# A transformer pair on one core: block-attention heads set between projection blocks, full-width attention tiles, a shorter rotary front

## The chip, the cores and the metric

The kernel runs on one core of one Trainium2 chip. The time is device microseconds (us) of one execution, smaller is better; given is the median of three runs. Engines: PE (TensorE; PEld is its weight load), DVE (VectorE), ACT (ScalarE), POOL (GpSimd) and SP, which issues loads.

## The reference

Two transformer blocks over 256 tokens of width 1024 (16 meta tokens stand before them as keys, 272 in all). The first block has latent attention (MLA, 8 heads, 64 plain and 32 rotary features), differential attention (4 heads of two maps) and a mixture of 16384 experts. The second has a hybrid mixer, cross attention over a memory of 256 and a convolutional FFN. What the change touches:

```
q = rmsnorm(c_q @ w_uq); k = rmsnorm([k_nope, k_rope])
q, k = [nope, rope(rotary part)]        # t1*cos - t2*sin, t1*sin + t2*cos
y_mla = softmax(q k^T * s + mask) v     # 8 heads, 272 keys
y_diff = (softmax(q1 k1^T) - lam * softmax(q2 k2^T)) v     # 4 heads
proj = h @ w_in_2                       # 3200 columns: conv 768, moba q,k,v 1536, gla 896
y_conv = c_b * dwconv(c_c * c_h);  y_moba = softmax(causal, alibi) v     # 8 heads
x = x + [y_conv, y_moba, y_gla] @ w_out_2
x = x + cross_attention(rmsnorm(x) * g)
```

## The kernel before, in words

Activations lie feature-major: 128 features on the partitions, 256 tokens (272 in the front) along the row. Every weight matrix is cut into blocks of 128x1024 that SP loads into `raw`, a ring of four (`RING`). Each block is split into two float32r parts: ACT makes `w_hi` (L717), and POOL or DVE, by `lo_owner`, makes `w_lo` (L588, L1219). `project` (L1926) multiplies a block with eight operand tiles, three products each (hi·hi, lo·hi, hi·lo), so a block is 24 passes of PE. Products go by turns to PSUM banks 0 and 1 and are taken from there by DVE or ACT (`bank_free`). Each engine's order is written out by hand; semaphores join them.

**Front** (`project_in`, 17 blocks of 272 columns). Between its blocks stand: the query product of the 8 MLA heads from `w_uq` (L2063), the values (`values`, L2027), the rotary turn of the queries by a constant matrix (`spread` with `rot`, L1970), the keys, four heads at a time in 64 columns (`keys`, L2035, twice), the turn of the shared rotary key (L2092), and the keys' sums of squares (L2096, L2098). POOL multiplies all queries with the cosines (L661); DVE multiplies the turned ones with the sines and adds (L1322, L1326), the same for the key (L1330, L1333). The memory's norm (L851, L1307) runs beside them.

**Attention** (`attention` on each engine, `walk` gives the steps). In step s PE computes `scores(s+1)` (L2178), `weigh(s-2)` (L2220) and `turn(s-1)` (L2198, transposes of the probabilities). DVE makes the row maximum (`soft_in`), the inverse of the sum and the lower part of a finished head (`finish`, L1442); ACT the exponential (L904), the copy of turned probabilities (L913) and the upper part of a head (`head_out`, L925); POOL scales by the inverse (`normalise`, L626). `key_tiles` cuts the 272 keys into tiles of 128, 128 and 16 rows, and transposes of a causal tile are cut to 32 rows. Values of an MLA, block ("moba") or cross head are 64 columns wide.

**Mixer** (`project_in2`, 25 blocks in the order `IN2_ORDER`). The gated linear attention ("gla") runs between the first blocks. The convolution on DVE (L1778 to L1786) follows blocks 16 to 18, the scores of the first two block heads stand after blocks 21 and 22, and the other steps of the eight heads come when all 25 blocks are done. Their outputs go into `x_op`, the operand that the 25 blocks read. Two pieces of output block 0 (`first_out2`) stand in the last two steps. Then come output blocks 0 to 7, the sum of squares (`mixed_sum`, L1961, L1963), the eight operand tiles of cross attention (`gained_hi`, L753 on ACT, `gained_lo`, L1250 on DVE) all behind the last output block, and the query blocks of cross attention.

## Time and profile before

| | |
|---|---|
| time, median of 3 runs | 1409.96 us (1407.91 to 1410.04) |
| the profiled execution | 1411.54 us, span 1409.4 us |
| busy | PE 98%, PEld 88%, DVE 69%, ACT 48%, POOL 53% of the span |
| mean granted PE clock | 0.993 |
| chain that ended last | PE 88%, DVE 5%, ACT 2%, POOL 2%, issue 2% |

The span is from the first to the last instruction; some 2 us lie around it. A row of the timeline gives start, length, engine, line, operation and shapes; 128*64 before the operand is the part of the array in use, rows by columns. One float32 matmul is two rows of PE. The length of a row holds the modelled end of its last matmul, so lengths are read here from one start to the next. In brackets stands the idle time ahead and what ended it.

### The profile page before, as it was taken

How to read it: one execution, taken by the hardware profiler on the slowest of the kernel's cores; microseconds unless marked ns; L12 is line 12 of the kernel's file. 1: busy time of each engine (PE TensorE's matmuls, PEld its weight loads, DVE VectorE, ACT ScalarE, POOL GpSimd, SP SyncE). 2: the span in 40 equal slices, each digit the busy share in tenths (PEclk: the TensorE clock that was granted, in tenths of full speed). 3: DMA queues.
4: the chain of work that ended last, by engine and by line, in shares of the span. 5: the costliest groups of instructions: out<-in, count | busy, mean ns of one | idle time of the engine just before them, and what ended most of it. 6: DMA issues, size and time to landing. Idle time of an engine off the chain costs nothing.

```text
span 1409.4 us, 28595 instructions
## 1 busy us (share of the span) xinstructions
PE 1377.3 (98%) x9810; PEld 1244.9 (88%) x9810; DVE 970.2 (69%) x1690; ACT 681.1 (48%) x1044; POOL 743.8 (53%) x606
## 2 busy tenths in 40 slices
PE   9999999999999999999999999999999988899997
PEld 8777689999999999988888888999999967799996
DVE  6724659999888888766666665544455754798886
ACT  6433665445555555533333333444465356555553
POOL 5423268888777667644444444444434535455441
PEclk9999999999999999999999999999999999999999
DMA  7511156667655555567777776555544513465552
GB/s 300 162 47 45 65 171 208 189 203 225 206 184 185 177 181 184 184 220 238 237 227 237 238 230 205 197 189 180 183 172 136 178 54 112 135 190 181 179 179 75
DMA packets 89801, 249.67 MB, mean 177 GB/s; under 512 B 9976, under 2 KB 35848, under 8 KB 89100
## 3 DMA queue, kind: packets, MB, share of 16 engines
q1 hardware_dynamic: 88260, 243.20, 53.3%
q10 hardware_dynamic: 1480, 5.65, 1.1%
q8 instruction: 40, 0.66, 0.2%
q14 instruction: 21, 0.17, 0.0%
HBM read 234.64 MB, written 15.25 MB: 177 GB/s over the span
## 4 chain that ended last, share of the span: by engine, by line
PE 88%; DVE 5%; ACT 2%; POOL 2%; issue 2%; DMA 0%; ACTq 0%; DVEq 0%; SPq 0%; POOLq 0%
PE ps L1926 45%; PE ps L2376 25%; PE ps L2363 4%; PE ps L2346 3%; POOL w_lo L588 2%; PE ps L2220 1%; PE ps L2178 1%; PE ps L2198 1%; PE ps L2148 1%; DVE w_lo L1219 1%; PE ps L2000 1%; PE ps L2035 1%; ACT w_hi L717 1%; PE ps L1941 1%; DVE big L1255 0%
## 5 line engine op out<-in xcount | busy, mean ns | idle before, releaser
L588 POOL TENSOR_TENSOR w_lo<-raw,w_hi 128x512 fp32r<-128x512 f32 x514 | 679.4, 1343 | 536.8 <-ACT w_hi L717 532.6
L1926 PE MATMUL ps<-x_op,w_hi 128*128 128x256 f32 (+1 forms) x3824 | 711.4, 287 | 6.4 <-DVE x_op L1250 3.3
L1926 PEld LDWEIGHTS ps<-x_op,w_hi 128*128 128x128 f32 x3824 | 597.0, 191 | 19.7 <-issue 9.0
L717 ACT ACTIVATE w_hi<-raw 128x1024 fp32r<-128x1024 f32 x399 | 420.0, 1055 | 273.5 <-PE ps L2376 206.4
L1926 PE MATMUL ps<-x_op,w_lo 128*128 128x256 f32 (+1 forms) x1912 | 541.2, 283 | 0.0
L1926 PEld LDWEIGHTS ps<-x_op,w_lo 128*128 128x128 f32 x1912 | 365.8, 191 | 0.0
L2376 PE MATMUL ps<-w_hi,h_op 128*128 128x512 f32 x1008 | 280.7, 395 | 0.0
L1219 DVE TENSOR_TENSOR w_lo<-raw,w_hi 128x1024 fp32r<-128x1024 f32 x141 | 183.3, 1300 | 83.4 <-ACT w_hi L717 82.9
L2376 PEld LDWEIGHTS ps<-w_hi,h_op 128*128 128x128 f32 x1008 | 187.4, 188 | 43.1
L2376 PE MATMUL ps<-w_lo,h_op 128*128 128x512 f32 x504 | 158.6, 395 | 0.0
L1621 DVE TENSOR_TENSOR work<-route_t,ps 128x1536 bf16<-128x1536 bf16 x64 | 112.3, 1754 | 8.7
L2376 PEld LDWEIGHTS ps<-w_lo,h_op 128*128 128x128 f32 x504 | 94.7, 188 | 23.0
L1648 DVE CAST h_op<-ps 128x256 fp32r<-128x256 f32 x128 | 54.4, 425 | 81.2 <-PE ps L2376 72.4
L1001 ACT ACTIVATE kv_mem<-ps 128x256 f32<-128x256 f32 x98 | 37.5, 383 | 133.1 <-PE ps L1926 133.1
L1617 DVE TENSOR_TENSOR route_t<-kept,ps 128x1024 bf16<-128x1024 f32 x64 | 78.2, 1222 | 30.9 <-PE ps L2346 27.1
L1641 DVE TENSOR_TENSOR ps<-work,big 128x256 f32<-128x256 f32 x124 | 54.3, 438 | 35.6 <-ACT work L1042 33.6
L2363 PE MATMUL ps<-h_op,w_hi 128*128 128x256 f32 x368 | 66.3, 280 | 1.7 <-DVE h_op L1856 1.7
L626 POOL TENSOR_TENSOR big<-big 128x256 f32<-128x256 f32 (+3 forms) x48 | 26.2, 567 | 70.5 <-DVE big L1417 70.5
L2363 PEld LDWEIGHTS ps<-h_op,w_hi 128*128 128x128 f32 x368 | 56.4, 188 | 2.1 <-DVE h_op L1856 1.2
L1650 DVE TENSOR_TENSOR h_op<-ps,h_op 128x256 fp32r<-128x256 f32 x128 | 54.4, 425 | 4.4
L2346 PE MATMUL ps<-work,route_t 128*128 128x128 bf16 x768 | 54.0, 220 | 0.2 <-DVE work L1621 0.2
L2363 PE MATMUL ps<-h_op,w_lo 128*128 128x256 f32 x184 | 51.7, 281 | 0.0
(332 smaller groups left out, 1264.7 us busy)
## 6 DMA issues: line engine op xcount, KB each, us to landing
raw<-blocks SPq DMA_DIRECT2D x403, 512.0 KB, 3.7
early_store<-kv_mem SPq DMA_DIRECT2D x96, 128.0 KB, 1.7
work<-early_store SPq DMA_DIRECT2D x96, 128.0 KB, 3.9
big<-consts SPq DMA_DIRECT2D x1, 1336.0 KB, 8.8
big<-consts ACTq DMA_DIRECT2D x1, 1336.0 KB, 5.4
big<-h_t ACTq DMA_DIRECT2D x4, 272.0 KB, 5.1
big<-bias_lines SPq DMA_DIRECT2D x8, 136.0 KB, 4.4
bias_lines<-bias_lines SPq DMA_DIRECT2D x1, 1056.0 KB
```

What stands on the lines that cost most here:

```text
L588: ins = pool.tensor_tensor(w_lo[:, s, half], raw[:, s, half], w_hi[:, s, half].bitcast(F32), ALU.subtract)
L717: act.activation(w_hi[:, s, :], raw[:, s, :], ACT.Copy).then_inc(sem("hi_done"), 1)
L1219: dve.tensor_tensor(w_lo[:, s, :], raw[:, s, :], w_hi[:, s, :].bitcast(F32), ALU.subtract).then_inc(sem("lo_dve"), 1)
L1617: dve.tensor_tensor(marks[:, m:m + 2], con("iota").unsqueeze(1).unsqueeze(1).to_broadcast([P, 2, 4, P]), routed[:, m:m + 2, tok].unsqueeze ...
L1621: dve.tensor_tensor(scaled[:, m], marks[:, 1].unsqueeze(1).to_broadcast([P, 3, 4, P]), routed[:, 3:6, tok].unsqueeze(3).to_broadcast([P, 3 ...
L1641: dve.tensor_tensor(weighted[:, b, :], a, G[:, bass.ds(chunk.value(), 1), :].rearrange("p e t -> p (e t)"), ALU.mult).then_inc(sem("act_us ...
L1648: dve.tensor_copy(h_op[:, b, 0, :], weighted[:, b, :]).then_inc(sem("act_hi"), 1)
L1650: dve.tensor_tensor(h_op[:, b, 1, :], weighted[:, b, :], h_op[:, b, 0, :].bitcast(F32), ALU.subtract).then_inc(sem("acts_ready"), 1)
L1926: mm = pe.matmul(ps[:, m_bank, 0:T], w, xp, start=(k == 0 and j == 0), stop=(k == last and j == 2))
L2346: mm = pe.matmul(ps[:, 2 + j % 2, P * k:P * k + P], marks[:, 2 * (j % 2), k, :], scaled[:, j % 2, r, k, :], start=(r == 0), stop=(r == 2))
L2363: mm = pe.matmul(out, w, x, start=(first and j == 0 and k % 2 == 0), stop=(last and j == 2), skip_group_check=True)
L2376: mm = pe.matmul(ps[:, 4 + 2 * t + half, :], h_op[:, b, h, rows], w[:, s, 512 * half:512 * (half + 1)], start=(first and j == 0), stop=Fal ...
```

## The change

- `w_uq` has 128 columns per head: 96 as before and the 32 rotary ones once more in turned order; the front's block 4 likewise. The turned features fall out of the products, so both multiplications with `rot` go. ACT copies the turned rows (32 partitions), DVE multiplies them with gain and signed sines, multiplies the straight ones with the cosines and adds, all on 32 partitions. POOL's multiplication goes. `w_uq` grows from 768 to 1024 KB.
- `keys` makes two heads per matmul, once; the keys' sums of squares take pairs. The gain of the plain key features moves into `key_scale`. The wait for the memory's root stands one matmul group later.
- Tiles of keys are always 128 wide: the third one overlaps the second and its values are zero in the overlap (`tail`). Transposes are 128x128, values 128 columns (a pair of heads; the half that is not wanted is not read).
- Mixer: `IN2_ORDER` brings the block heads' queries and keys ahead of the convolution's inputs. The scores of heads 0 and 1 stand after blocks 14 and 15; each of the eight steps of attention has one projection block (17 to 24) in it. Block heads write into `first_op`, an own buffer, and both halves of bank 7. A head's `weigh` waits until the one before it has been read (`outputs_out`). The convolution stands in steps 6 to 8 of DVE. Output block 0 is cut into tiles (6,7), (2,3), (4), (0,1), (5). POOL and ACT split one block per step.
- Cross attention's operand tiles are made one by one behind each residual.

```diff
-IN2_ORDER = [24, 18, 19, 20, 21, 22, 23, 14, 15, 16, 17, 0, 1, 2, 3, 4, 5, 6, 10, 7, 11, 8, 12, 9, 13]
+IN2_ORDER = [24, 18, 19, 20, 21, 22, 23, 14, 15, 16, 17, 6, 10, 7, 11, 2, 8, 12, 3, 9, 13, 4, 5, 0, 1]
...
-                yield j, min(P, units[u]["keys"] - P * j), first, at
+                yield j, min(P * j, units[u]["keys"] - P), first, at
...
+        def out_at(o, rows=slice(0, P), first=0):
+            if 0 <= o - HEADS - DH < MH:
+                return ps[rows, 7, (o % 2) * NQ + first:(o % 2 + 1) * NQ]
+            return ps[rows, 7 if o % 2 == 0 else 1, first:NQ]
...
-            pool.tensor_tensor(rope_a[:, :, 0:NQ], q_mla,
...
+            for i in range(MH):
+                los(B_FILL + 2 + i, B_FILL + 3 + i)
+                normalise(U_MOBA + i, U_MOBA + i + 1)
...
+            act.activation(flat2(rope_p), banks(4, 4)[QK:P, :], ACT.Copy).then_inc(sem("q_raw"), 1)
...
+            for i, (s, p, o) in enumerate(walk(U_MOBA, U_X)):
+                if s is not None and i >= 2:
+                    soft(s)
+                his(min(B_FILL + 4 + i, B_OUT2 + RING))
+                if i == 3:
+                    mix_hi(0, y_gla, 6)
+                if i == 9:
+                    mix_hi(1, conv_y, 0)
+                if o is not None:
+                    head_out(o)
+                if p is not None:
+                    probs_out(p)
...
                 act.wait_ge(sem("bank_free"), M_OUT2 + j + 1)
+                gained_hi(R_XATTN, "xattn", (j,))
                 squares(res[:, j, :], j, NQ)
...
+            for i, (s, p, o) in enumerate(walk(U_MOBA, U_X)):
+                if i >= 3:
+                    finish(U_MOBA + i - 3)
+                if p is not None and i >= 3:
+                    inverse(p)
+                if s is not None and i >= 2:
+                    soft_in(s)
+                if 1 <= i <= 8:
+                    evacuate_in2(16 + i)
+                if i == 5:
+                    mix_lower(0, y_gla, 6)
...
-                pe.wait_ge(sem("y_hi"), o - 1)
-                pe.wait_ge(sem("y_ready"), outputs_read(o))
+                one = 0 < o - HEADS - DH <= MH
+                pe.wait_ge(sem("y_hi"), o - 1 + one)
+                pe.wait_ge(sem("y_ready"), outputs_read(o) + one)
...
+            def fill_moba(s, p):
+                if s is not None:
+                    project_in2(17 + s - U_MOBA)
+                elif p is not None:
+                    pe.wait_ge(sem("mix_lo"), 1)
+                    first_out2((6, 7))
+                    moba_done(4)
+                    first_out2((2, 3))
+                else:
+                    moba_done(6)
+                    first_out2((4,))
+            attention(U_MOBA, U_X, 2, fill_moba)
+            pe.wait_ge(sem("mix_lo"), 2)
+            first_out2((0, 1))
+            moba_done(MH)
+            first_out2((5,))
```

**Where instructions move.** PE in the front, between projection blocks 7 and 12 (`...` stands for blocks); before:

```order
L1970 MATMUL ps<-big 96x512 x4
...
L2027 MATMUL ps<-big 16x512 x2
...
L2035 MATMUL ps<-big 64x272 x8
...
L2092 MATMUL ps<-big 96x272
L2096 MATMUL ps<-big,ones 8x272
L2098 MATMUL ps<-big 8x272 x8
```

and now:

```order
L2040 MATMUL ps<-big 128x512 x2
...
L2046 MATMUL ps<-big 128x272 x8
...
L2101 MATMUL ps<-big,ones 8x272
L2103 MATMUL ps<-big 8x272 x4
```

Both turns are gone; the group of key products stood twice and stands once, at full width; the sums are halved.

PE in one step of the block heads, between the scores of one head and the transposes of another; before:

```order
L2178 MATMUL ps<-big 128x128
L2178 MATMUL ps<-big 128x256
L2220 MATMUL ps<-big 64x256
L2220 MATMUL ps<-big 64x128
L2198 MATMUL ps<-kept,big 128x128 x3
```

and now, with the 24 passes of a projection block between scores (L2184) and `weigh` (L2226):

```order
L2184 MATMUL ps<-big 128x128
L2184 MATMUL ps<-big 128x256
L1944 MATMUL ps<-x_op,w_hi 128x256 x2
L1944 MATMUL ps<-x_op,w_lo 128x256
...
L2226 MATMUL ps<-big 128x256
L2226 MATMUL ps<-big 128x128
L2204 MATMUL ps<-kept,big 128x128 x3
```

The same step is longer by a block, and there are eight such blocks fewer ahead of the heads.

DVE in step 6 of the block heads now: `finish` (L1450), inverse, row maximum, a lower part (L1227), a block taken from PSUM (L1725), then half the convolution (L1800 to L1806), which before stood between blocks 17 and 18 without a head beside it:

```order
L1450 TENSOR_TENSOR first_op<-ps,first_op 64x256
L1425 RECIPROCAL big<-big 128x2
L1408 SCALAR_TENSOR_TENSOR big<-big,ps 128x128
L1408 SCALAR_TENSOR_TENSOR big<-big,ps 128x256
L1417 TENSOR_REDUCE big<-big 128x1 x2
L1419 TENSOR_SCALAR big<-big 128x2
L1227 TENSOR_TENSOR w_lo<-raw,w_hi 128x1024
L1725 SCALAR_TENSOR_TENSOR big<-ps,big 128x256
L1800 TENSOR_TENSOR big<-big 128x512
L1804 TENSOR_SCALAR big<-big,par 128x256
L1806 SCALAR_TENSOR_TENSOR big<-big,par 128x255
L1806 SCALAR_TENSOR_TENSOR big<-big,par 128x254
```

The convolution moved from the projection's stretch into the heads' steps, behind the row maximum.

## Rows read from the trace of the kernel before

**Rows 1.** DVE's groups, 1086 to 1128: busy, mean ns, idle ahead and its end.

```profile
L1219 DVE TENSOR_TENSOR w_lo<-raw,w_hi 128x1024 fp32r<-128x1024 f32 x7 | 9.2, 1308 | 0.1
L1719 DVE SCALAR_TENSOR_TENSOR big<-ps,big 128x256 f32<-128x256 f32 x14 | 5.9, 423 | 10.9 <-PE ps L1926 10.9
```

**Rows 2.** Busy time by stretch: length, PE, PEld, DVE, ACT, POOL, clock, DMA.

```profile
45.00:97.20 52.20, 50.82 (x305) 37.61 (x303) 23.00 (x18) 21.53 (x35) 15.88 (x9) 1.00 0.32 107
1127.30:1151.20 23.90, 19.84 (x93) 12.45 (x92) 14.24 (x47) 13.51 (x43) 6.37 (x12) 0.86 0.07 23
1141.10:1147.90 6.80, 6.22 (x22) 4.08 (x21) 2.32 (x9) 2.95 (x10) 2.31 (x5) 0.50 0.00 0
```

**Rows 3.** Timeline of PE in the front, projection blocks mostly left out.

```profile
48.02 3.70 PE L2027 MATMUL ps<-big 128*128 128x512 f32 x8 [0.92 <-ACT big L851]
...
54.58 3.60 PE L1970 MATMUL ps<-big 96*96 96x512 f32 x8
57.61 0.81 PE L1926 MATMUL ps<-x_op,w_hi 128*128 128x272 f32 x2
...
66.17 3.89 PE L2035 MATMUL ps<-big 128*64 128x272 f32 x16
...
80.25 0.69 PE L2092 MATMUL ps<-big 32*96 32x272 f32 x2
...
81.42 3.83 PE L2098 MATMUL ps<-big 64*8 64x272 f32 x16
```

**Rows 4.** Timeline of DVE and of POOL in the same stretch.

```profile
54.82 6.72 DVE L1219 TENSOR_TENSOR w_lo<-raw,w_hi 128x1024 fp32r<-128x1024 f32 x1
...
54.46 4.74 POOL L661 TENSOR_TENSOR big<-big 96x2048 f32<-96x2048 f32 x1 [2.80 <-issue]
```

**Rows 5.** Timeline of PE ahead of attention and in one MLA step.

```profile
115.25 1.04 PE L2277 MATMUL ps<-kept,big 128*128 128x128 f32 x8
116.13 1.28 PE L1977 MATMUL ps<-ones 128*128 128x128 f32 x10
...
129.91 1.14 PE L2220 MATMUL ps<-big,work 128*64 128x256 f32 x6
130.99 1.00 PE L2198 MATMUL ps<-kept,big 128*128 128x128 f32 x5
131.92 0.97 PE L2178 MATMUL ps<-big 128*128 128x144 f32 x4
```

**Rows 6.** Timeline of PE: projection block 12, steps of the block heads, output block 0.

```profile
1087.14 0.48 PE L1926 MATMUL ps<-x_op,w_hi 128*128 128x256 f32 x2
...
1090.10 0.40 PE L1926 MATMUL ps<-x_op,w_hi 128*128 128x256 f32 x2
...
1129.17 0.92 PE L2178 MATMUL ps<-big 64*128 64x128 f32 x4
1130.02 0.86 PE L2220 MATMUL ps<-big 128*64 128x256 f32 x4
1130.81 0.55 PE L2198 MATMUL ps<-kept,big 128*128 128x128 f32 x3
...
1139.51 0.55 PE L2198 MATMUL ps<-kept,big 128*128 128x128 f32 x3 [1.29 <-POOL big L626]
...
1151.28 0.50 PE L1926 MATMUL ps<-x_op,w_hi 128*128 128x256 f32 x2 [0.93 <-DVE x_op L1442]
```

**Rows 7.** Timeline of DVE in the convolution, and of POOL beside it.

```profile
1104.10 1.01 DVE L1783 SCALAR_TENSOR_TENSOR big<-big,par 128x255 f32<-128x255 f32 x2
...
1105.92 2.97 DVE L1783 SCALAR_TENSOR_TENSOR big<-big,par 128x255 f32<-128x255 f32 x2
...
1105.89 2.72 POOL L588 TENSOR_TENSOR w_lo<-raw,w_hi 128x512 fp32r<-128x512 f32 x2 [2.83 <-ACT w_hi L717]
```

**Rows 8.** Timeline of PE: first query blocks of cross attention, and the scores behind.

```profile
1175.77 0.47 PE L1926 MATMUL ps<-x_op,w_hi 128*128 128x256 f32 x2 [0.16 <-DVE x_op L1250]
...
1180.62 1.14 PE L2178 MATMUL ps<-big 64*128 64x256 f32 x8
```

More of the change, by code:

```diff
@@ L852, in _ @@
             evacuate_in(6)
+            act.activation(xf[0:QK, 0:HEADS * NQ], banks(4, 4)[0:QK, :], ACT.Square).then_inc(sem("q_squares"), 1)
             evacuate_in(7)
@@ L1796, in _ @@
+            mix_lower(1, conv_y, 0)
+            finish(U_X - 1)
             for k in range(KT):
@@ L1914, in arrived, with project @@
                 pe.wait_ge(*rest_taken(n))
-            def project(n, m_bank, T=NQ, free=None, ready=None, tiles=range(KT), last=KT - 1, x=x_k):
-                if 0 in tiles:
+            def project(n, m_bank, T=NQ, free=None, ready=None, tiles=range(KT), last=KT - 1, x=x_k, first=0):
+                if first in tiles:
                     arrived(n)
@@ L1925, in project @@
                     for j, (w, xp) in enumerate(parts(n.mod(RING), k * P, k * P + P, x(0, k, T), x(1, k, T))):
-                        mm = pe.matmul(ps[:, m_bank, 0:T], w, xp, start=(k == 0 and j == 0), stop=(k == last and j == 2))
+                        mm = pe.matmul(ps[:, m_bank, 0:T], w, xp, start=(k == first and j == 0), stop=(k == last and j == 2))
                 if last in tiles:
@@ L2022, in values @@
             def values(t):
-                rows = min(P, NK - P * t)
+                key = min(P * t, NK - P)
                 if t == 2:
@@ L2026, in values, with keys @@
                 for k in range(2):
-                    mm = pe.matmul(ps[0:rows, 2 + t % 2, :], ckvn[:, k, P * t:P * t + rows], w_ukv[:, k, 512:1024],
-                                   start=(k == 0), stop=(k == 1))
+                    mm = pe.matmul(ps[:, 2 + t % 2, :], ckvn[:, k, key:key + P], w_ukv[:, k, 512:1024], start=(k == 0), stop=(k == 1))
                 mm.then_inc(sem("v_product"), 1)
-            def keys(w):
-                for h in range(4):
+            def keys():
+                for pair in range(HEADS // 2):
                     for k in range(2):
-                        a = NOPE * (4 * w + h)
-                        mm = pe.matmul(ps[0:NOPE, 4 + h, 0:NK], w_ukv[:, k, a:a + NOPE], ckvn[:, k, :], start=(k == 0), stop=(k == 1))
+                        mm = pe.matmul(ps[:, 4 + pair, 0:NK], w_ukv[:, k, P * pair:P * pair + P], ckvn[:, k, :], start=(k == 0), stop=(k == 1))
                 mm.then_inc(sem("k_product"), 1)
@@ L2271, in _ @@
             for t in range(3):
-                rows = min(P, NK - P * t)
+                key = min(P * t, NK - P)
                 if t == 2:
@@ L2537, in cross_out, with first_heads @@
                     mm.then_inc(sem("block_used"), 1)
-            def first_heads(part):
+            def first_heads(s, p):
+                if s is not None:
+                    return
+                part = 0 if p is not None else 1
                 pe.wait_ge(sem("y_ready"), HEADS + DH + MH + 2)
@@ L2616, in constants @@
     half = ROPE // 2
-    rot = np.zeros((QK, QK))
-    for j in range(half):
-        rot[NOPE + half + j, NOPE + j] = -1.0
-        rot[NOPE + j, NOPE + half + j] = 1.0
-    put("rot", rot)
     freq = np.float32(10000.0) ** (-np.arange(half, dtype=np.float32) / np.float32(half))
@@ L2703, in layout @@
     put("final", lay("final_norm_g_2"))
+    put("tail", (np.arange(P) >= 2 * P - (NK - P)).astype(np.float32))
+    for k, source in enumerate(("mla_qk_norm_q", "mla_qk_norm_k")):
+        put("qkp", np.concatenate([np.zeros(NOPE, np.float32), lay(source)[0][turned]]), k)
     for name, source in (("dq", "diff_q_norm"), ("dk", "diff_k_norm"), ("gla", "gla_norm_g_2")):
```

255 lines of the change are left out of this document (118 added, 137 removed).

## The prediction

> **What bounds the kernel now.** I read the page's engines and chain first: PE is busy 98% of the span and carries 88% of the chain that ended last (both in the table of the profile), so a change pays where it takes passes from PE or a wait from in front of it. Then the groups of DVE in the mixer's projection: its evacuation of a block waited 10.9 us for PE and never the reverse, and one lower part costs it 1.3 us, one evacuation 0.42 [rows 1]. Then the busy time by stretch: in the front PE works 50.8 of 52.2 us while DVE works 23.0 and POOL 15.9; in the stretch of the block heads it works only 19.8 of 23.9, at a mean granted clock of 0.86, and within it from 1141.1 to 1147.9 at 0.50, that is at 1.2 GHz [rows 2]. So the front is short of nothing but passes, and the block heads are the one place where PE starves and then also runs slowly. Last come the timelines, for the length of every piece that changes. All sums are against the profiled execution of 1411.54 us; the median of the runs is 1.6 us below it, and I take that off at the end.
>
> **A. Front ahead of attention: -10.1 us.** Removed from PE, each from its start to the next one's: the turn of the queries, 54.58 to 57.61, 3.0 us; one of two groups of key products, 16 rows from 66.17, 3.8 us; the turn of the shared key, 80.25 with one more product behind it, 0.6; half of the keys' sums, which ran from 81.42 for 3.8 us, 1.9 [rows 3]. The values waited 0.92 us for ACT's root (L851) [rows 3]; the wait now stands behind a group of half that length, 1.6 us, which covers it. Together 10.3. The products with `w_uq` keep their time though their columns go from 96 to 128: a row's length follows what streams through, since 16 rows take 3.89 us at 64 columns and 16 take 3.83 at 8 [rows 3]. Added off PE: a copy on ACT (2048 columns, which took POOL 4.74 us with a second input [rows 4]; ACT works 21.5 of 52 us [rows 2], so it has room for even that); three operations of DVE on 32 partitions in place of two on 96, and `key_scale` with a gain more. DVE has 29 us free of 52 here [rows 2], so they cost nothing but the last one, where PE waited for it closely; I charge 0.2 for this (0 to 0.5). POOL's 4.74 us multiplication goes; beside it one lower part on DVE took 6.72 us instead of 1.3 [rows 4, 1]. PE did not wait for it, hence 0, but the cover grows. `w_uq` is 256 KB longer; the DMA engines are busy to 0.32 at 107 GB/s here [rows 2], so this is 2.4 us of a queue that idles most of the time; 0, at worst a quarter of it, 0.6. Bounds of A: -9.0 to -10.8.
>
> **B. Attention front: -4.8 us.** A step of an MLA head lasts 2.9 us on PE, from `weigh` at 129.91 over the transposes at 130.99 and the scores at 131.92 to 132.8 [rows 5]. Its pure work at full width: one row of 128x128 takes 0.11, eight taking 0.88 from 115.25 to 116.13 [rows 5]. Five transposes are then 0.55; scores of 416 columns in two rows each 0.69; `weigh` of 448 columns 0.75; in all 2.0. Before, the transposes took 0.93 and `weigh` 1.08 since array shapes changed at 64 columns, 32 rows and 16 rows. I do not book the whole 0.9. `weigh` of a head waits for the output of the one before it to be read, which waits for ACT's `head_out` and DVE's `finish`, and the transposes for POOL's scaling. No row parts what of the 0.9 is this loop and what shape, so I take the middle, 2.5: 8 x 0.4 = 3.2. The four differential heads lose about 0.4 each in the same way: 1.6. Bounds of B: 0, if the other engines' chain sets the step already, to -8.8, if all changes of shape go.
>
> **C. Mixer: -7.5 us.** Before, from block 12's first pass (1087.14) to the end of output block 0 it takes 65.6 us: its second half begins at 1151.28, and 12 passes of 0.12 end it at 1152.7 [rows 6]. Eight groups of three passes take 1087.14 to 1090.10, 2.9 a block [rows 6]. Now PE has there: 13 blocks, 37.8; eight scores of 0.85 (1129.17 to 1130.02), 6.8; eight `weigh`, now at the shape of the projection, hence 768 columns in all at 0.11 per 128, 0.65 instead of 0.79, 5.1; eight times three transposes of 0.11, 2.6; output block 0, 2.9 [rows 6, 5]. Sum 55.2. What is not hidden: the last two heads have no projection block behind them, only pieces of output block 0, and the loop `weigh`, `head_out`, `finish` that ended in waits of 1.29 and 0.93 [rows 6] stands once more at the tail; 1.1. DVE is late in step 6: its share per head is 14.24 us over eight, 1.8 [rows 2], with 0.42 and 1.3 for evacuation and lower part 3.5, and half the convolution adds 1.3 to 1.5 alone and up to 3.7 beside POOL (a pair of L1783 takes 1.01 us alone, 2.97 beside a 2.72 us lower part of POOL [rows 7]). That makes 7 us in a step in which PE has 2.9 + 0.85 + 0.65 + 0.33 = 4.7 of work, with a step of slack in the PSUM banks; 1.7. Total 58.1, so -7.5. The half clock goes too: with a projection block in every step PE has no row of short waits such as it had before 1141. Bounds of C: -5.0 with every step 0.3 longer and the tail at 2, -9.2 with nothing late but the tail.
>
> **D. Cross attention: -0.8 us.** The first one and a half query blocks ran 1175.77 to 1180.62, 4.85 us for 36 passes that cost 4.32, and waited 0.16 for DVE's lower parts of the operand [rows 8]. With the tiles made behind each residual both losses go, and a little of the wait ahead. Against it: `squares` now stands behind a gain on ACT, which I put at one operation of such a size, 0.4 us [rows 1]. Bounds of D: -2 to +0.3.
>
> **Sum.** -10.1 - 4.8 - 7.5 - 0.8 = -23.2: 1388.3 for a profiled execution, 1386.8 against the median. Below, "the same" means within 0.2%, 2.8 us, about what a measurement of this kernel can tell from no change.
>
> **Rivals.** *R1, DVE sets the block heads' step.* DVE now carries evacuation, lower parts, convolution and soft heads in one queue, and POOL's lower parts run beside them. If contention as in [rows 7] meets it in most steps (3.5 becomes 5.5, PE's 4.7 is exceeded by 0.8 in six of the eight), C gains 2.7 only: 1391.6. For it: 2.97 against 1.01. Against it: POOL works 6.4 of 23.9 us here [rows 2], and its share per step only grows by half a lower part. The Trainium skill, "SBUF — State Buffer", section on the two separate sides, says that DVE with two SBUF inputs and GpSimd exclude each other for a whole instruction; by that rule DVE waits out each lower part of POOL that it meets, and [rows 7] agree. Chance 0.14.
>
> *R2, attention's front is set by the other engines.* DVE, ACT and POOL pass one head's data in turn, and PE only fills in; then a shorter PE step becomes a longer wait ahead of transposes or `weigh`, and B is 0: 1391.6. For it: the 0.93 us of five transposes hold at most 0.4 of shape changes and may be such a wait already [rows 5]. Against it: no release is named at these rows. Chance 0.10.
>
> *R3, slower.* `finish` stands first in DVE's step; until PE has weighed and ACT has copied the head, the lower part and the evacuation behind it stand still, and PE's next block needs both. One such round, a head's share, lower part and evacuation, is 3.5 us by C; PE sits out nothing as long as it is under 4.7 plus the 2.9 of one block that is ready ahead. From 7.6 us on PE waits each step. To lose the 23 us of all terms, eight steps would have to be 7.6 + 3.5 us, 11 us each; at 11.5 us the result is 1413. Lower parts of 6.72 us [rows 4] in place of 1.3 would come near. Chance 0.04.
>
> *R4, the change doesn't take out what it says.* Both turns and one key group are gone from the order of instructions, so this leaves only a front whose loads or ACT become late: half of A, 1392. Chance 0.04.
>
> **Numbers.** The forecast, all four terms about as worked out, has 0.68. It, R1, R2 and R4 lie between 1378 and 1398: the low end has B and C each some 4 us better than booked, the high end R1 and R2 together with A at its lower bound. Own range of the forecast: 1380 to 1391. Faster by over 0.2%: 0.94; the same 0.02; slower 0.04.
>
> **What the profile of the changed kernel would show.** A: no row of the turns, one group of key products, PE's work ahead of attention about 10 us shorter, no row of DVE's lower part near 6.7 us beside it. B: 2.5 us from `weigh` to `weigh`; 2.9 speaks for R2, 2.1 for my low end. C: granted clock 1.0 across the block heads, a step of 4.7 to 5 us, short waits at the transposes, a wait at projection block 22 or 23 behind DVE's evacuation. A step over 5.5 us with PE's wait ended by DVE in most steps is R1; over 7.6, R3. D: 36 passes in 4.3 us. I would be wrong most likely by the attention front, whose loop I could not separate from its shape changes, or by the half clock, if PE falls to 1.2 GHz elsewhere.

## The result, and the profile after

The changed kernel takes 1392.63 us (median of 4 runs, 1391.68 to 1393.47) against 1409.58 us for the kernel before (4 runs, 1407.91 to 1410.04); the ratio is 0.9882 with a 95% interval of 0.9865 to 0.9899. It is 17.0 us faster where 23.2 were forecast. It lies within the stated range of 1378 to 1398, but outside the forecast's own range of 1380 to 1391. The profiled executions differ by 18.1 us (1411.54 to 1393.47, spans 1409.4 and 1391.3), and their difference can be laid out stage by stage, by the starts of the same matmuls on PE in both:

| stretch of PE | before | after | change | booked |
|---|---|---|---|---|
| start to the first sum over ones in the front (19.30; 16.58) | 19.30 | 16.58 | -2.7 | none |
| from there to attention's first memory transposes (115.25; 101.60) | 95.95 | 85.02 | -10.9 | A, -10.1 |
| attention, to the residual's operand (182.25; 163.67) | 67.00 | 62.07 | -4.9 | B, -4.8 |
| experts, to block 12 of the mixer (1087.14; 1069.13) | 904.89 | 905.46 | +0.6 | none |
| block 12 to the end of output block 0 (1152.72; 1131.44) | 65.58 | 62.31 | -3.3 | C, -7.5 |
| output blocks 1 to 7, to the sum of squares (1174.47; 1154.49) | 21.75 | 23.05 | +1.3 | D |
| to cross attention's scores (1183.90; 1164.81) | 9.43 | 10.32 | +0.9 | D, -0.8 |
| the rest | 225.5 | 226.5 | +1.0 | none |

The first line is no effect of the change, as the repeated profiles below show. From block 12 to the end the profiles take 322.3 us before and 322.2 after, and the repeated pair below takes 322.3 and 322.2 again: what the mixer gains is lost behind it. In these profiles the whole gain stands ahead of the experts.

The page of the changed kernel, busy time by engine: all shares as before within one per cent.

```profile
PE 1358.2 (98%) x9776; PEld 1245.2 (89%) x9776; DVE 972.9 (70%) x1691; ACT 681.7 (49%) x1045; POOL 738.4 (53%) x605
```

PE in the front, which answers to [rows 3]:

```profile
59.19 3.84 PE L2046 MATMUL ps<-big 128*128 128x272 f32 x16
...
69.56 2.00 PE L2103 MATMUL ps<-big 128*8 128x272 f32 x8
```

One group of key products stands where two stood, with as many rows as one of them had, and the sums of squares take 2.0 instead of 3.8 us.

PE in two steps of MLA, to be set against [rows 5]:

```profile
115.24 1.01 PE L2226 MATMUL ps<-big,work 128*128 128x256 f32 x6
116.09 0.74 PE L2204 MATMUL ps<-kept,big 128*128 128x128 f32 x5
116.67 0.87 PE L2184 MATMUL ps<-big 128*128 128x144 f32 x4
117.46 1.11 PE L2226 MATMUL ps<-big,work 128*128 128x256 f32 x6
118.48 0.76 PE L2204 MATMUL ps<-kept,big 128*128 128x128 f32 x5
```

From one `weigh` to the next it is 2.22, then 2.42 us, against 2.9. The transposes' share went from 0.93 to 0.58, that of the scores from 0.90 to 0.79.

The mixer by stretch (length, PE, PEld, DVE, ACT, POOL, clock, DMA), to be set against [rows 2]: the heads' steps with a block in each, the heads' tail, the first query blocks of cross attention, and a piece of its attention.

```profile
1077.90:1116.90 39.00, 39.00 (x284) 34.94 (x284) 26.49 (x62) 20.38 (x48) 18.87 (x21) 1.00 0.33 110
1117.20:1131.40 14.20, 9.95 (x68) 8.46 (x66) 11.55 (x23) 6.54 (x15) 6.42 (x7) 1.00 0.38 119
1154.50:1161.50 7.00, 7.00 (x40) 6.53 (x40) 2.88 (x4) 2.50 (x5) 2.52 (x2) 0.76 0.62 204
1174.00:1177.50 3.50, 3.50 (x18) 3.10 (x18) 0.21 (x1) 2.01 (x4) 3.45 (x4) 0.63 0.00 0
```

For 39 us PE does not miss a beat; then, in the tail of 14.2 us, it works 9.95 and DVE 11.55. The half clock has left the heads' steps, but stands now in the query blocks and in cross attention.

PE in the middle of the heads' steps, in their tail and behind the output blocks (projection rows mostly left out), to be set against [rows 6, 8]:

```profile
1096.68 0.81 PE L2226 MATMUL ps<-big 128*128 128x256 f32 x4
1097.34 0.49 PE L2204 MATMUL ps<-kept,big 128*128 128x128 f32 x3
1097.76 0.92 PE L2184 MATMUL ps<-big 64*128 64x128 f32 x4
1101.58 0.81 PE L2226 MATMUL ps<-big 128*128 128x256 f32 x4
...
1120.51 0.89 PE L2226 MATMUL ps<-big 128*128 128x256 f32 x4 [0.21 <-DVE first_op L1450]
...
1124.86 0.89 PE L2226 MATMUL ps<-big 128*128 128x256 f32 x4 [0.93 <-DVE first_op L1450]
1126.91 0.55 PE L2204 MATMUL ps<-kept,big 128*128 128x128 f32 x3 [1.16 <-POOL big L633]
...
1128.04 0.92 PE L2226 MATMUL ps<-big 128*128 128x256 f32 x4 [0.23 <-ACT big L917]
1130.36 0.50 PE L1944 MATMUL ps<-first_op,w_hi 128*128 128x256 f32 x2 [1.40 <-DVE first_op L1456]
...
1146.29 0.51 PE L1944 MATMUL ps<-first_op,w_hi 128*128 128x256 f32 x2 [0.47 <-POOL w_lo L595]
...
1154.49 0.70 PE L1974 MATMUL ps<-big,ones 128*128 128x256 f32 x2 [2.27 <-POOL big L618]
...
1161.52 1.14 PE L2184 MATMUL ps<-big 64*128 64x256 f32 x8
```

A step is 4.90 us (1096.68 to 1101.58) without a wait. In the tail some 4 us of waits stand in brackets, ended by DVE's `finish`, POOL's scaling and the lower part of the convolution's output (L1456). All PE waits from block 12 to the end of output block 0 add up to 4.3 us, before to 4.4: they have moved to the tail and are not fewer. Ahead of the sum of squares PE waits 2.27 us for POOL (1.33 before), and it waits 0.47 for a lower part of POOL once more.

### The profile page after: what moved, and what is told of

It is laid out like the page before. It is cut to its first block, busy times and chain, and to the rows that moved or that the text cites. A ratio compares the mean times of both kernels' runs of the same rounds, so it can differ in the third digit from the quotient of the medians.

```text
span 1391.3 us, 28517 instructions
## 1 busy us (share of the span) xinstructions
PE 1358.2 (98%) x9776; PEld 1245.2 (89%) x9776; DVE 972.9 (70%) x1691; ACT 681.7 (49%) x1045; POOL 738.4 (53%) x605
## 4 chain that ended last, share of the span: by engine, by line
PE 88%; DVE 6%; ACT 2%; issue 2%; POOL 1%; DMA 1%; ACTq 0%; DVEq 0%; SPq 0%; POOLq 0%
PE ps L1944 47%; PE ps L2382 25%; PE ps L2369 4%; PE ps L2352 3%; PE ps L2184 1%; PE ps L2226 1%; ACT w_hi L720 1%; DMA raw<-blocks 1%; PE ps L2152 1%; PE ps L2204 1%; DVE w_lo L1227 1%; DVE big L1249 1%; PE ps L1959 1%; DVE big L1263 1%; PE ps L2320 1%
## 5 line engine op out<-in xcount | busy, mean ns | idle before, releaser
L1944 PE MATMUL ps<-x_op,w_hi 128*128 128x256 f32 (+1 forms) x3696 | 689.2, 287 | 5.4 <-DVE x_op L1258 3.5
L1944 PEld LDWEIGHTS ps<-x_op,w_hi 128*128 128x128 f32 x3696 | 577.5, 191 | 18.6 <-issue 9.0
L1944 PE MATMUL ps<-x_op,w_lo 128*128 128x256 f32 (+1 forms) x1848 | 523.4, 283 | 0.0
L1944 PEld LDWEIGHTS ps<-x_op,w_lo 128*128 128x128 f32 x1848 | 353.7, 191 | 0.0
L1227 DVE TENSOR_TENSOR w_lo<-raw,w_hi 128x1024 fp32r<-128x1024 f32 x141 | 180.3, 1279 | 88.2 <-ACT w_hi L720 87.7
```

The costliest lines, as they stand in the source:

```text
L1227: dve.tensor_tensor(w_lo[:, s, :], raw[:, s, :], w_hi[:, s, :].bitcast(F32), ALU.subtract).then_inc(sem("lo_dve"), 1)
L1944: mm = pe.matmul(ps[:, m_bank, 0:T], w, xp, start=(k == first and j == 0), stop=(k == last and j == 2))
```

## The experiments

All times are medians, and the stretches are read from each run's own profile. The stretch "mixer" is from block 12's first pass to the sum of squares: 87.3 before, 85.4 after.

**The changed kernel again.** No edit.

> The changed kernel once more, unaltered, for what repeats. Theory 1 (the clock's dips have places): the stretch at half clock stands again behind the last output block (36 passes of the first query blocks in about 6.1 us, where 4.3 would be full clock), PE idles again some 4 us between 1117 and 1131, and the front has none. Theory 2 (the dips fall by chance): the query blocks' length differs by over 1 us from 6.1, or the front of projections behind 13 us shows a half-clock stretch of 1.5 us or more, and the time moves with it. Time 1392.6 +- 1.

Measured: 1392.09 us (1390.18 to 1395.12). The mixer takes 85.36 us, to the hundredth what the first profile of this kernel has, with nearly the same waits (0.21, 0.98, 1.16, 1.41, 2.48) and the same 6.1 us for 36 passes. The front is another matter. Busy time by stretch of this run (first the front, then the query blocks):

```profile
12.00:16.00 4.00, 3.86 (x17) 3.86 (x18) 3.95 (x5) 1.78 (x4) 2.87 (x2) 0.50 1.00 397
1156.00:1162.00 6.00, 5.91 (x32) 5.55 (x33) 2.68 (x4) 2.60 (x5) 2.56 (x3) 0.72 0.69 230
```

So theory 1 holds for the mixer, theory 2 for the front: the same program runs from 12 to 16 us at 1.2 GHz in one execution and at 2.4 GHz in another. The profiled execution is the slowest of the four at a mean clock of 0.993, the fastest has 0.998, so the later dips need not stand in every execution either.

**The kernel before again.** No edit.

> The kernel before once more, for what repeats in it. If the half-clock stretch of the front (12 to 18 us) falls by chance, its length may differ by 1 us or more from the first profile of it; the time from block 12's first pass to the sum of squares is 87.3 us with the dip in the block heads at 1141, about 85.3 if that dip falls elsewhere. The waits for POOL's scaling in the heads' steps (0.65, 1.29) and the 1.33 ahead of the sum of squares repeat within 0.2 us.

Measured: 1410.52 us (1408.39 to 1411.82). Its front and its block heads by stretch:

```profile
12.00:16.00 4.00, 3.92 (x30) 3.81 (x30) 3.96 (x6) 2.29 (x3) 2.98 (x2) 1.00 1.01 405
1140.00:1148.00 8.00, 7.42 (x31) 5.01 (x30) 2.54 (x10) 3.59 (x12) 2.31 (x5) 0.57 0.01 2
```

This time the front of the kernel before has the full clock, and its first sum over ones starts at 16.87 us instead of 19.30. The -2.7 in the first line of the table is therefore no effect of the change. Like is compared with like by the stretch from that sum to attention's first transposes: with the dip ahead of it 95.96 us before and 84.28 after, without it 96.91 and 85.02, so the change takes 11.7 or 11.9 us and not 10.9. Some 0.7 to 1.0 us of the dip's cost is thus made up again before attention. The mixer takes 87.30 us, and its dip repeats, with the waits of 0.66 and 1.30 ahead of it.

**Projection blocks ahead of the heads again.** The interleaving alone is undone.

```diff
-            project_in2(16)
+            project_in2(16, 9)
...
                 if s is not None:
-                    project_in2(17 + s - U_MOBA)
+                    return
...
+            los(B_FILL + 2, B_OUT2 + 2)
             for i in range(MH):
-                los(B_FILL + 2 + i, B_FILL + 3 + i)
...
             soft(U_MOBA + 1)
+            his(B_OUT2 + 2)
...
-            evacuate_in2(16)
+            evacuate_in2(18)
             inverse(U_MOBA + 1)
+            evacuate_in2(24)
```

> The changed kernel with the interleaving alone undone: projection blocks 17 to 24 stand ahead of the heads' steps again, with their evacuations and lower parts; own buffer, halves of bank 7, full-width tiles, the cut of output block 0 and the convolution in steps 6 to 8 are kept. Theory 1 (a block in each step covers the loop over the other engines): PE waits in most steps, 4 us or more in the mixer, time 3.5 to 6 us above the changed kernel's, 1396 to 1398. Rival (the wait at the tail is the same either way and the interleaving moves it only): within 1.5 us of the changed kernel's.

Measured: 1398.57 us (1396.94 to 1399.43), mixer 91.8 us, 6.5 more than with a block in each step. PE in its steps, and the stretch by clock:

```profile
1113.91 0.89 PE L2228 MATMUL ps<-big 128*128 128x256 f32 x4
1114.94 0.55 PE L2206 MATMUL ps<-kept,big 128*128 128x128 f32 x3
1115.42 0.92 PE L2186 MATMUL ps<-big 64*128 64x128 f32 x4
1117.75 0.89 PE L2228 MATMUL ps<-big 128*128 128x256 f32 x4 [1.41 <-ACT big L917]
1118.90 0.79 PE L2206 MATMUL ps<-kept,big 128*128 128x128 f32 x3 [0.27 <-POOL big L633]
1119.62 1.65 PE L2186 MATMUL ps<-big 64*128 64x128 f32 x4
...
1128.73 1.62 PE L2228 MATMUL ps<-big 128*128 128x256 f32 x4 [1.45 <-DVE first_op L1451]
```

```profile
1118.00:1132.00 14.00, 12.28 (x42) 9.16 (x42) 10.64 (x34) 7.14 (x23) 3.77 (x8) 0.54 0.00 1
```

After one wait of 1.41 us every group takes nearly double (scores 1.65 for 0.92), until blocks come again. Of the 6.5 us only 0.8 is more waiting (5.1 us against 4.3 to the end of output block 0, in five places of over 0.25 us and not in most steps, as theory 1 had it); by far the most is the clock, at half speed for some 15 us. What the blocks in the steps keep up is the clock, more than they cover waits. The time to the end shows even less of it: this profile has no dip behind the mixer, and from block 12 to the end it takes 325.8 us against 322.2.

**Without the taps of the convolution.** This version leaves the filter out, so its output is not the reference's.

```diff
-                if i in (6, 7):
-                    t = i - 6
-                    w = [pcol("scw", 3 * t + j) for j in range(3)]
-                    step(dve.tensor_scalar(conv_y[:, t, :], conv_u[:, t, :], w[2], pcol("scb", t), ALU.mult, ALU.add))
-                    for back in (1, 2):
-                        step(dve.scalar_tensor_tensor(out=conv_y[:, t, back:NQ], in0=conv_u[:, t, 0:NQ - back], scalar=w[2 - back],
-                                                      in1=conv_y[:, t, back:NQ], op0=ALU.mult, op1=ALU.add))
...
-                    dve.tensor_tensor(flat2(conv_y), flat2(conv_y), flat2(proj2[:, 0:2, :]), ALU.mult)
+                    dve.tensor_tensor(flat2(conv_y), flat2(conv_u), flat2(proj2[:, 0:2, :]), ALU.mult)
```

> Leaves out the three taps of the convolution per half on DVE (2.8 us of DVE in steps 6 and 7 of the block heads); the last product reads the product of the inputs in place of the filtered one. Theory 1 (the convolution stands in front of finish and makes the heads' last steps late): PE's idle time from projection block 23 to the end of output block 0, 4.3 us in the changed kernel, falls to 2.5 or less, time 1390 to 1391. Rival (the loop of weigh, head_out, finish and the scaling at the tail, where no projection block is left to cover it): idle time stays at 3.6 or more, time within 0.7 us of the changed kernel's.

Measured: 1390.9 us (1389.43 to 1392.85), 1.2 below the changed kernel in the same series; mixer 83.81, 1.55 less. The waits on `finish` (0.21 and 0.98) are gone, one of 0.57 for ACT's copy stands in their place, and those of 1.16 for POOL, 0.23 and 1.41 at the end stay. The tail's waits still add up to 3.4 us, between the bounds of the two theories. So both have a part: some 1.5 us are the convolution's, 2.5 and more are not.

**The convolution's first half early.**

```diff
-IN2_ORDER = [24, 18, 19, 20, 21, 22, 23, 14, 15, 16, 17, 6, 10, 7, 11, 2, 8, 12, 3, 9, 13, 4, 5, 0, 1]
+IN2_ORDER = [24, 18, 19, 20, 21, 22, 23, 14, 15, 16, 17, 6, 10, 7, 11, 2, 4, 8, 12, 9, 13, 3, 5, 0, 1]
...
-                            pe.wait_ge(sem("bank_free"), M_IN2 + (13, 15, 18, 21)[h // 2])
+                            pe.wait_ge(sem("bank_free"), M_IN2 + (13, 15, 19, 21)[h // 2])
...
-                if i == 6:
-                    dve.wait_ge(sem("bank_free"), M_IN2 + 23)
-                    step(dve.tensor_tensor(flat2(conv_u), flat2(proj2[:, 2:4, :]), flat2(proj2[:, 4:6, :]), ALU.mult))
-                if i in (6, 7):
-                    t = i - 6
+                if i in (2, 6):
+                    t = i // 6
+                    dve.wait_ge(sem("bank_free"), M_IN2 + (17, 23)[t])
+                    step(dve.tensor_tensor(conv_u[:, t, :], proj2[:, 2 + t, :], proj2[:, 4 + t, :], ALU.mult))
+                if i in (2, 7):
+                    t = i // 7
```

> The inputs of the convolution's first half are projected as blocks 15 and 16, and that half (product and taps) is done in step 2 of DVE, where it has 12 of 39 us free; the second half's product stays in step 6, its taps stand in step 7. All work is kept. Theory 1: as without taps in its size: 1.5 to 2 us of idle time go, time 1390.5 to 1391.5, if step 2 has the room; PE has no new wait in steps 2 to 4. Rival (the loop at the tail): no change within 0.7 us. A third way: step 2 becomes late itself and PE waits ahead of weigh or turn there, 1 us lost.

Measured: 1389.78 us (1389.26 to 1390.31), the range all but below that of the changed kernel in the same series; mixer 83.62, 1.74 less, with all work kept. PE in its tail:

```profile
1123.24 0.89 PE L2227 MATMUL ps<-big 128*128 128x256 f32 x4 [0.40 <-DVE first_op L1450]
1125.29 0.55 PE L2205 MATMUL ps<-kept,big 128*128 128x128 f32 x3 [1.16 <-POOL big L633]
1126.42 0.92 PE L2227 MATMUL ps<-big 128*128 128x256 f32 x4 [0.23 <-ACT big L917]
1128.75 0.51 PE L1945 MATMUL ps<-first_op,w_hi 128*128 128x256 f32 x2 [1.41 <-DVE first_op L1456]
```

The wait of 0.21 is gone and that of 0.93 has become 0.40, as without the taps; step 2 had the room. What is left are waits of the last two heads for ACT, DVE and POOL, which no projection block covers; the two longest of them are looked into at R1 below.

**Gains behind all output blocks again.** The last part of the change is undone, on ACT and on DVE.

```diff
                 act.wait_ge(sem("bank_free"), M_OUT2 + j + 1)
-                gained_hi(R_XATTN, "xattn", (j,))
                 squares(res[:, j, :], j, NQ)
+            act.wait_ge(sem("block_used"), B_XQ)
+            gained_hi(R_XATTN, "xattn", range(KT))
...
-                if k:
-                    gained_lo(R_XATTN, "xattn", (k - 1,))
-            gained_lo(R_XATTN, "xattn", (KT - 1,))
+            dve.wait_ge(sem("bank_free"), M_XQ)
+            gained_lo(R_XATTN, "xattn", range(KT))
```

> Only the last part of the change is undone: the operand tiles of cross attention are made behind all eight output blocks again. Theory 1 (the gains between the output blocks delay ACT's upper parts and squares and through them POOL): PE's wait ahead of the sum of squares falls from 2.27 to about 1.3 us; the first query blocks wait as before the change (4.85 us for 36 passes), at full clock: time 1390 to 1391. Rival (that wait comes from elsewhere, the gain is that PE finds the tiles ready): the wait stays above 2, the query blocks lengthen, time 1393 to 1394.

Measured: 1390.64 us (1389.68 to 1392.3). The wait ahead of the sum of squares and the stretches of its profile:

```profile
1155.61 0.70 PE L1974 MATMUL ps<-big,ones 128*128 128x256 f32 x2 [1.54 <-POOL big L618]
```

```profile
1128.00:1134.00 6.00, 5.24 (x23) 4.47 (x22) 3.25 (x6) 1.41 (x4) 2.59 (x2) 0.53 0.51 178
1155.00:1162.00 7.00, 6.10 (x42) 5.48 (x44) 5.71 (x11) 5.57 (x12) 2.96 (x3) 1.00 0.42 151
```

The wait falls from 2.27 to 1.54, the one of 0.47 goes, and the query blocks take 4.86 us, all as theory 1 had it. But the half clock did not vanish: it stands at 1129 to 1135, right behind the heads' tail, where this stretch had run at full clock. Mixer and query blocks together, block 12 to cross attention's scores at 1165.03, take 95.1 us against 95.7 (1069.13 to 1164.81), and what follows takes 1.4 us less, as cross attention has no dip here. In all the version without D is 1.5 us faster than the changed kernel of the same series, by medians whose ranges overlap.

**The wait filled.** Ten matmuls on ones in it.

```diff
+            keep_warm(10, 6)
             mixed_sum(R_XATTN)
```

> Ten matmuls of 128x128 on ones (2.1 us of PE, results unused) stand ahead of the sum of squares behind the last output block, where PE waits 2.3 us for POOL and then runs the query blocks at half clock. Theory 1 (the half clock there comes from that idle time): granted clock stays 1.00 from 1154 to 1162, 36 passes take 4.4 instead of 6.1 us, time 1.7 us shorter, 1390.5 +- 1. Theory 2 (the dip follows the row of waits in the heads' tail at 1120 to 1130 and is only late): the dip stays there or shifts within the next 10 us, time as the changed kernel's, 1392.3 +- 1.

Measured: 1392.5 us (1391.85 to 1392.96), no gain. Its stretches:

```profile
1154.00:1162.00 8.00, 7.74 (x60) 7.06 (x60) 5.08 (x6) 3.22 (x6) 4.68 (x4) 1.00 0.60 176
1188.00:1192.00 4.00, 3.80 (x13) 2.67 (x13) 0.92 (x1) 1.11 (x2) 2.82 (x3) 0.57 0.38 130
```

Theory 1 holds where the matmuls stand: full clock, 36 passes in 4.6 us. The sum of squares comes no later (mixer 85.4 us) and the scores of cross attention stand 94.2 us behind block 12 instead of 95.7. The time does not follow: a dip stands 30 us further on, in cross attention, whose waits are not filled. That is not the whole of it, since from block 12 to the end this profile is still 2.4 us shorter than the first one of the changed kernel, while the front behind the first sum and the experts, which the edit does not touch, are 1.0 and 0.7 longer; whether that is chance is open.

**Squares ahead of gains on ACT.**

```diff
-                gained_hi(R_XATTN, "xattn", (j,))
                 squares(res[:, j, :], j, NQ)
+                gained_hi(R_XATTN, "xattn", (j,))
```

> ACT squares a residual tile before it makes the operand's upper part of it, in place of after. Theory 1 (the gain ahead of the square makes POOL's sum late, 0.4 to 0.5 us in each output block): PE's wait ahead of the sum of squares falls from 2.3 to 1.8 or less, the wait of 0.47 for POOL's lower part ahead of an output block goes; 0.5 to 1 us shorter. Rival (the lower and upper parts of weights are what is late): both waits stay within 0.15 us.

Measured: 1391.52 us (1390.54 to 1392.56). Both waits stay (0.48, 2.28), so the order of square and gain is not what delays POOL. But its profile has the full clock behind the same wait:

```profile
1154.00:1162.00 8.00, 5.94 (x46) 5.67 (x48) 4.95 (x6) 3.10 (x6) 4.55 (x4) 1.00 0.50 164
```

An idle time of 2.3 us can be followed by the half clock, and need not be.

**Three edits together**: first half early, squares first, wait filled.

> Three edits together: the first half of the convolution in step 2, squares ahead of gains, and ten matmuls on ones ahead of the sum of squares. If the three costs are separate (1.7 by the convolution, 0.5 to 1 by the squares, 1.7 by the clock) the time is 3.5 to 4.4 us below the changed kernel, 1388 to 1389. If the clock only moves its dip elsewhere, 1390.

Measured: 1389.83 us (1389.0 to 1390.46), no better than the early half alone. Its profile has no dip between 16 and 1380 us, and yet the fill brings nothing measurable. Neither the 3.5 nor the 4.4 us came in the time: of the three costs only the convolution's is solid there. By stretch the profile has them (block 12 to cross attention's scores 92.3 us, 93.8 with the early half alone), but its experts take 1.3 us more than there, and no run tells why.

**Gains last on ACT, with the first half early.**

```diff
+            his(B_OUT2 + 3)
             for j in range(KT):
-                his(B_OUT2 + j + (3 if j < KT - 1 else 4))
+                if j == KT - 1:
+                    his(B_OUT2 + j + 4)
...
-                gained_hi(R_XATTN, "xattn", (j,))
                 squares(res[:, j, :], j, NQ)
+                if j < KT - 1:
+                    his(B_OUT2 + j + 4)
+                gained_hi(R_XATTN, "xattn", (j,))
```

> The convolution's first half early, and on ACT behind each output block the square first, then the next block's upper part, then the gain. Theory 1 (ACT's gain ahead of the next upper part makes POOL's lower parts and sums late): the wait of 0.48 for POOL's lower part goes, the one ahead of the sum of squares falls from 2.28 to 1.5 or less; 1 to 1.3 us below the run with the early half alone, 1388.5. Rival (POOL is late by its own chain of lower parts and additions): both waits stay.

Measured: 1388.54 us (1388.26 to 1389.56), ratio to the kernel before 0.9841, interval 0.9821 to 0.9861. The wait of 0.48 is gone, so it was the upper part behind the gain that made POOL late there. The other one moves little:

```profile
1152.32 0.70 PE L1979 MATMUL ps<-big,ones 128*128 128x256 f32 x2 [2.06 <-POOL big L618]
```

This is the fastest version of the study, 1.2 us below the early half alone by medians of different series, and by its median below both kernels.

**Narrow values in `weigh`.** 64 columns of values as before the change; transposes stay wide.

```diff
-                pair = slice(P * (h // 2), P * (h // 2) + P)
+                rows = slice(0, P) if x["kind"] == "diff" else slice(64 * (h % 2), 64 * (h % 2) + 64)
+                pair = slice(64 * h, 64 * h + 64)
...
-                    mm = pe.matmul(out_at(o, first=first), v, probs_t[:, o % 2, at:at + NQ - first],
+                    mm = pe.matmul(out_at(o, rows, first=first), v, probs_t[:, o % 2, at:at + NQ - first],
```

> weigh reads 64 columns of values and writes 64 rows for MLA, block and cross heads, as before the change; transposes stay at 128x128. Theory 1 (what the attention front gained is changes of array shape): each MLA step grows by about 0.2 us (weigh of 0.95 to 1.08 and one change behind it), 1.6 in all, the block heads by 0.15 each, hidden nowhere: time 2 to 3 us longer than the changed kernel's. Theory 2 (the loop over ACT, DVE and POOL sets an MLA step of 2.4): the front stays within 0.4 us, and only the block heads' 1.2 us show.

Measured: 1396.28 us (1394.57 to 1396.75), 3.8 above the run with the filled wait of the same series. PE in two MLA steps:

```profile
115.47 1.00 PE L2227 MATMUL ps<-big,work 128*64 128x256 f32 x6
116.40 0.76 PE L2204 MATMUL ps<-kept,big 128*128 128x128 f32 x5
117.00 0.87 PE L2184 MATMUL ps<-big 128*128 128x144 f32 x4
117.80 1.00 PE L2227 MATMUL ps<-big,work 128*64 128x256 f32 x6
```

A step is 2.33 us, and attention in all 62.42 against 62.05: 0.4 us, not 1.6. The narrow `weigh` takes 0.93 to 1.05 from start to start, the wide one 0.84 to 1.06. So what attention's front gained comes with the transposes' width (0.93 to 0.6 for five in both versions), hardly with the values'. The mixer takes 88.15 us, 2.8 more than the changed kernel, 1.8 of it a dip behind the heads' tail (129 passes in 17.75 us instead of 15.94); the values' width pays there, some 1 us without the dip: a step of the block heads takes 5.18 us instead of 4.90, with a `weigh` of 0.79 for 0.65 and longer transposes and blocks behind the changes of shape.

## Why the forecast was right in sign and too large in size

The number fell into the stated range in part by luck. A and B were booked at 14.9 us and gave 16.7. C and D were booked at 8.3, and from block 12 to the end the profiles show 0.1. The first error made up for some of the second. That the result stands near the 1391.6 to 1392 of R1, R2 and R4 does not speak for them: the stages do not show what they describe.

**A, the front: right in mechanism, booked too low.** Booked 10.1 with bounds of 9.0 and 10.8, found 11.7 and 11.9 between profiles that are alike in the front's clock. Each removed piece shows with about its length. More came off than was booked: the key products went from 7.64 to 3.48 us where 3.8 was taken off, and the values from 4.96 to 4.35 since their third tile has the full shape, for which nothing was booked. Of the -13.6 with which attention begins in the first pair, 1.5 to 1.9 is clock: the profile of before, on which the prediction rested, had its front at half clock from about 12 to 18 us, and that comes and goes in either kernel. [Rows 2] began at 45 us and did not show it.

**B, attention's front: right in size, with some luck in the reason.** 4.9 for 4.8. The step is 2.2 to 2.7 us, around the 2.5 that was taken as the middle between pure work (2.0) and present (2.9). But the other engines' loop, for which the half was held back, did not bind: the MLA steps show no wait at their transposes or `weigh` over 0.1 us, so 2.2 to 2.7 is PE's own work, and the 2.0 was too low. Rival R2 falls there; in the differential heads 0.9 us of waits is new (0.28, 0.20, 0.42). The other part of the reason, the width of `weigh`, is worth 0.4 us by its undoing; the rest comes with the transposes.

**C, the mixer: the steps right, the work and the tail mis-sized, the clock wrong.** From block 12 to the end of output block 0 it took 62.3 us where 58.1 was booked (the terms add up to 58.0). (1) Work: without its waits PE takes 58.1 us for what was booked at 55.2. Blocks take 2.97 to 3.06 behind the scores' 64 rows, 1.4 more in all; `weigh` takes 0.9 more, most of it in the tail, and the transposes, 0.42 and more for three, 0.6. (2) Waits: booked 1.1 for the loop and 1.7 for DVE being late; they add up to 4.3. The runs assign 1.5 to the convolution, near the 1.7. Of the rest about 2.0 is DVE and POOL in each other's way, which the sum had for the convolution only and otherwise left to rival R1; by the lengths below, the loop itself has some 0.8, less than the 1.1. (3) "The half clock goes too" is the step that failed. It left the heads' steps, as said, and this is most of the 3.3 us that the stretch gained (an estimate: from 1140.8 to 1148.6 the groups of before took 2.7 us more than the same groups do at full clock). It came back in the query blocks (6.1 us for 36 passes, 4.6 at full clock in six versions, booked 4.3) and in cross attention (the rest takes 226.5 us, 225.1 in the versions without a dip there): 1.5 and 1.4 us, about as much as had been won. The prediction had named this as one of two ways to be wrong, without a price.

**D: wrong in sign.** Booked -0.8, found +2.2 to cross attention's scores. The terms written down (0.53 and 0.16 gained, 0.4 lost) come to -0.3 only; the other half, "a little of the wait ahead", was never worked out, and that wait grew. Of what was found, 1.5 is the clock of the query blocks and 1.4 is waits, against 0.6 that was gained around and in those blocks, as booked. The waits come since ACT's gain stands ahead of the upper part of the next block, and POOL's lower parts and additions behind it are late: 0.47 plus 0.9 us. Undoing D alone takes these waits back to none and 1.54. The prediction charged one operation of 0.4 for the last block; it had to be charged where ACT feeds POOL. Of the remaining 2.06 of the wait ahead of the sum of squares 1.0 can be read from the trace: POOL's last addition there takes 1.71 us, 0.73 to 0.75 elsewhere, beside a lower part of DVE, and in the kernel before 1.70. The rest was not settled.

**The rivals.** R1 fell in its own form: DVE did not set the steps, which run 39 us without a wait. But contention of the kind of [rows 7] is there, in places that repeat. In the steps it stays hidden. DVE and POOL in the changed kernel, step 5 of the heads:

```profile
1114.60 1.00 DVE L1419 TENSOR_SCALAR big<-big 128x2 f32<-128x2 f32 x1
```

```profile
1114.28 3.60 POOL L595 TENSOR_TENSOR w_lo<-raw,w_hi 128x512 fp32r<-128x512 f32 x2
```

The small operation takes 0.17 us in five of the eight steps and 1.0 to 1.1 beside POOL in three. By the Trainium skill, "SBUF — State Buffer", section "Who interferes with whom", a tensor_scalar can enter a mode that takes the port pair shared with GpSimd, and the later of the two then waits for the other's whole instruction. By that rule, the trace agrees: POOL had begun 0.3 us earlier, and its first half ended at 1115.57, DVE's operation at 1115.60.

In the tail it is not hidden. DVE's lower part of the gla output and that of the convolution's output, two operations of one shape, and POOL beside the second:

```profile
1110.17 0.68 DVE L1456 TENSOR_TENSOR first_op<-big,first_op 128x512 fp32r<-128x512 f32 x1
...
1128.54 1.77 DVE L1456 TENSOR_TENSOR first_op<-big,first_op 128x512 fp32r<-128x512 f32 x1 [0.81 <-ACT first_op L934]
```

```profile
1128.50 1.26 POOL L595 TENSOR_TENSOR w_lo<-raw,w_hi 128x512 fp32r<-128x512 f32 x1
```

POOL's scaling of two heads, the second time behind a lower part of DVE that ran from 1124.83 to 1126.03:

```profile
1120.52 0.97 POOL L633 TENSOR_TENSOR big<-big 128x128 f32<-128x128 f32 x2 [2.64 <-DVE big L1425]
...
1124.99 1.87 POOL L633 TENSOR_TENSOR big<-big 128x128 f32<-128x128 f32 x2 [3.50 <-DVE big L1425]
```

DVE's operation began 0.04 us behind POOL's and takes 1.1 us more than its like; PE's wait of 1.40 hangs on it. POOL's scaling takes 0.9 us more; PE's wait of 1.16 hangs on that. Both lengths stand within 0.02 us in all ten profiles that have the blocks in the steps. So about 2.0 of the tail's 4.3 us of waits is this (an estimate from the lengths; no run moves the lower parts away to test it), and R1's mechanism was missing from C's sum at two places, not in most steps.

R4 falls, since A came whole, and R3, since no step of the block heads comes near 7.6 us. R3's sum was also off: it takes the head start of one block off every step, while a head start helps only once. By its own numbers, steps of 7.6 us, 2.9 above PE's 4.7, would already have cost the 23 us.

## To carry to other kernels

Spreading attention steps between long products works as long as there is a product left for each step; look at the last two steps first, for waits on the other engines are paid in full there. In these steps it also matters what DVE and POOL do at one time: keep a long lower part of one away from the operation of the other that PE waits for, and compare that operation's length with the same one elsewhere. Work of a side engine that is moved next to a loop belongs into the steps that have idle time on that engine, and a step added to the engine that feeds another belongs behind the feeding. Do not book the end of a half-clock stretch as a gain before a second profile shows it gone, and compare two profiles from the first microsecond and to the last, stage by stage: a dip that falls by chance can hide or fake up to 3 us, and a gain in one stage can be lost in the next, as all of C was here.

## What the chip showed that was not expected

- The clock's dip to 1.2 GHz moved rather than went. From the mixer on it stood at 1140 in the kernel before (twice), at 1156 and 1174 in the changed kernel (twice), at 1155 and 1173 without the taps, at 1153 with the early half, at 1129 with gains behind and with narrow values, at 1118 with blocks ahead, in cross attention at 1188 with the wait filled, and nowhere before 1380 with squares first, though the waits were the same there, nor with the three edits or with gains last. Where it falls repeats for the two programs that were profiled twice; a small edit shifts it. Why, these runs do not tell.
- Filling an idle time with matmuls on ones kept the clock at 1.00 there and gained nothing in the time (1392.5 against 1392.6 us in another series).
- The front's dip behind 12 us falls by chance in the same program (clock 0.50 or 1.00 from 12 to 16 us). It moves the first sum over ones by 2.4 to 2.7 us, and attention's start by 1.5 to 1.9.
- Five transposes of which two are cut to 32 rows took 0.93 us, five full ones 0.58 to 0.70. `weigh` at 64 columns took about as long as at 128 in attention (0.93 to 1.05 against 0.84 to 1.06), and longer in the block heads' steps (0.79 against 0.65).
- Operations of DVE and POOL that overlapped stretched each other by up to a whole instruction at the same two places of the tail in all ten profiles with blocks in the steps: 1.77 us for 0.68 on DVE, 1.30 for 0.40 on POOL.
